# Turned blocks copied inside SBUF by the weights' queue, in a hybrid SSD and attention encoder block

## What is computed

```python
h = rms_norm(x, g_mix)
proj = h @ w_in                         # z, xbc, dt, q, k, v, gate_a, gate_b
y_ssm = mamba2_bidir(z, xbc, ...)       # conv, two scans, times silu(z), grouped rms_norm
q, k = apply_rope(rms_norm(q)), apply_rope(rms_norm(k))
y_attn = gqa_bidir_blocks(q, k, v)
merged = sigmoid(gate_a) * (y_ssm @ w_ssm_up) + sigmoid(gate_b) * (y_attn @ w_attn_up)
x = x + merged @ w_out
x = x + square(relu(rms_norm(x, g_mlp) @ w_mlp_in)) @ w_mlp_out
return rms_norm(x, g_final)
```

## Time and profile before

| | us |
|---|---|
| median of 3 runs | 1610.12 |
| lowest and highest | 1608.63, 1610.78 |
| the profiled execution's own time | 1609.39 |
| its span, first to last instruction | 1607.3 |
| PE busy in it | 1595.4 |
| DVE, ACT, POOL busy in it | 1278.8, 927.99, 79.2 |

### The profile page before, as it was taken

One profiled execution on the slowest core, in us unless ns is written; L12 is line 12 of the kernel. 1 busy time (PEld: TensorE's weight loads), 2 busy tenths in 40 slices (PEclk: granted clock), 3 DMA queues, 4 the chain that ended last, 5 costly groups with the idle time before them and its releaser, 6 DMA issues.

```text
span 1607.3 us, 20614 instructions
## 1 busy us (share of the span) xinstructions
PE 1595.4 (99%) x7984; PEld 1349.2 (84%) x7984; DVE 1278.8 (80%) x1521; ACT 928.0 (58%) x1264; POOL 79.2 (5%) x67
## 2 busy tenths in 40 slices
PE   9999999999999999999999999999999999999998
PEld 7888888888888888888888888888888888888886
DVE  7978877888767688876666667999899988998893
ACT  7665566665666545554445555665566655655562
POOL 3000000000000134000000000000000000000000
PEclk9999999999999999999999999999999999999999
DMA  7665656665688776545877875558645863686461
GB/s 272 202 201 184 201 183 211 197 198 185 196 244 238 231 225 200 172 145 181 244 265 235 278 228 178 181 171 266 188 133 200 275 192 123 204 281 214 143 244 53
DMA packets 144993, 327.93 MB, mean 204 GB/s; under 512 B 10944, under 2 KB 19328, under 8 KB 144768
## 3 DMA queue, kind: packets, MB, share of 16 engines
q1 hardware_dynamic: 129376, 302.21, 58.5%
q10 hardware_dynamic: 15520, 24.41, 5.2%
HBM read 316.55 MB, written 10.03 MB: 203 GB/s over the span
## 4 chain that ended last, share of the span: by engine, by line
PE 95%; DVE 2%; issue 1%; DMA 1%; ACT 0%; POOL 0%; POOLq 0%; SPq 0%; ACTq 0%
PE G L1835 17%; PE G L1836 17%; PE G L1837 17%; PE G L1844 13%; PE S L1844 7%; PE G L1848 6%; PE S L1835 4%; PE S L1836 4%; PE S L1837 4%; PE S L1848 4%; PE S L1962 1%; DMA raw<-in_w_in 1%; DVE wlo L1108 1%; PE S L1990 0%; PE S L1939 0%
## 5 line engine op out<-in xcount | busy, mean ns | idle before, releaser
L668 ACT ACTIVATE whi<-raw 128x1024 fp32r<-128x1024 f32 x395 | 416.6, 1059 | 396.4 <-PE G L1837 230.4
L1108 DVE TENSOR_TENSOR wlo<-raw,whi 128x1024 fp32r<-128x1024 f32 x395 | 483.3, 1238 | 132.1 <-ACT whi L668 130.5
L1835 PE MATMUL G<-whi,a_both 128*128 128x512 f32 x768 | 300.0, 391 | 2.5 <-DVE wlo L1108 2.0
L1837 PE MATMUL G<-whi,a_both 128*128 128x512 f32 x768 | 299.0, 389 | 0.0
L1836 PE MATMUL G<-wlo,a_both 128*128 128x512 f32 x768 | 299.0, 389 | 0.0
L1844 PE MATMUL G<-a_both,whi 128*128 128x512 f32 x640 | 201.5, 396 | 0.0
L1835 PEld LDWEIGHTS G<-whi,a_both 128*128 128x128 f32 x768 | 144.2, 188 | 34.0 <-issue 2.8
L1837 PEld LDWEIGHTS G<-whi,a_both 128*128 128x128 f32 x768 | 144.2, 188 | 30.2
L1836 PEld LDWEIGHTS G<-wlo,a_both 128*128 128x128 f32 x768 | 144.2, 188 | 28.9
L1848 PEld LDWEIGHTS G<-a_both,wlo 128*128 128x128 f32 x640 | 120.2, 188 | 28.3
L1835 PE MATMUL G<-whi,b_hi 128*128 128x512 f32 x342 | 133.5, 390 | 0.0
(11 more groups left out here) (313 smaller groups left out, 2689.1 us busy)
## 6 DMA issues: line engine op xcount, KB each, us to landing
raw<-in_w_in SPq DMA_DIRECT2D x208, 512.0 KB, 4.4
raw<-in_w_mlp_in SPq DMA_DIRECT2D x74, 512.0 KB, 4.6
raw<-in_w_mlp_out SPq DMA_DIRECT2D x74, 512.0 KB, 4.9
gates<-in_w_mlp_in SPq DMA_DIRECT2D x54, 512.0 KB, 4.2
gates<-in_w_mlp_out SPq DMA_DIRECT2D x54, 512.0 KB, 4.8
raw<-in_w_ssm_up SPq DMA_DIRECT2D x32, 512.0 KB, 3.8
raw<-in_w_attn_up SPq DMA_DIRECT2D x32, 512.0 KB, 4.5
raw<-in_w_out SPq DMA_DIRECT2D x32, 512.0 KB, 5.2
```

The lines of the kernel that those rows point to most:

```text
L668: act.activation(high(m), piece(n), ACT.Copy).then_inc(hi_made, 1)
L1108: dve.tensor_tensor(low(m), piece(n), high(m).bitcast(F32), ALU.subtract).then_inc(lo_made, 1)
L1835: pe.matmul(out_ap, hi[:, k, cols], w_hi, start=start, stop=False)
L1837: return pe.matmul(out_ap, lo[:, k, cols], w_hi, start=False, stop=stop)
```

## The change

The two functions on ACT are gone, and the tensor `block_rows` with them. SP copies square row i to group j with a transfer of its own, from SBUF to SBUF: 32 partitions of 1 KB each, 32 KB, sixteen for a round, in four groups of four (one group for each j). SP does a group behind the load of a piece: it keeps a table `BESIDE` of the side work of every piece and, after issuing the load of piece n, does what belongs to piece n-7. So a z round has its groups at p 5, 6, 7 and p 0 of the next window, rope at p 6, 7, 0, 1, merged and residual at p 0, 1, 2, 3. A group waits for `blocks_turned`, the first of a round also for `lined` (or, for rope, `r_lo`), which tells that the last round's squares have been read. The count `s_across` (256 a round) takes the place of `s_put` and `s_got`: ACT waits for it before it puts the squares in order, DVE before it turns the next round. ACT gets one more wait, at p 2 of `residual`, for `taken`.

```diff
+SP_LAG = 7
+        def across(rnd, j, src, dst):
+            d = BLOCK_ROUNDS.index(rnd)
+            sp.wait_ge(blocks_turned, d + 1)
+            for i in range(4):
+                sp.dma_start(dst[Q * j:Q * (j + 1), i, :, :, :].rearrange("p c b t -> p (c b t)"),
+                             src[Q * i:Q * (i + 1), j, :, :, :].rearrange("p c b t -> p (c b t)")
+                             ).then_inc(s_across, 16)
+        def zgate(p, j):
+            if p == 5 and j:
+                sp.wait_ge(lined, j)
+            if p >= 5:
+                across(TS_Z + j, p - 5, blocks, turned_to)
+        def zturned(p, j):
+            if p == 0:
+                across(TS_Z + j, 3, blocks, turned_to)
...
+        def merged(p, j):
+            if j + TS_MERGED in ON_PE:
+                return
+            if p == 0:
+                sp.wait_ge(lined, BLOCK_ROUNDS.index(j + TS_MERGED))
+            if p < 4:
+                across(j + TS_MERGED, p, blocks, turned_to)
...
                 sp.dma_start(dst, src).then_inc(landed[piece_slot(n)], 16)
+                if n >= SP_LAG:
+                    then, done_beside = BESIDE[n - SP_LAG]
+                    for name, at in done_beside:
+                        if name in table:
+                            table[name](then, at)
...
-        def put_blocks(rnd, src=blocks[:, :, :, :, :]):
-            d = BLOCK_ROUNDS.index(rnd)
-            act.wait_ge(blocks_turned, d + 1)
-            act.dma_start(block_rows[d], src.rearrange("p j c b t -> p (j c b t)")).then_inc(s_put, 16)
-        def get_blocks(rnd, dst=turned_to):
-            d = BLOCK_ROUNDS.index(rnd)
-            act.wait_ge(s_put, 16 * (d + 1))
-            if d:
-                act.wait_ge(lined, d)
-            rows = block_rows[d].rearrange("(i w) (j x) -> j w i x", i=4, j=4)
-            for j in range(4):
-                act.dma_start(dst[Q * j:Q * (j + 1), :, :, :, :].rearrange("w i c b t -> w i (c b t)"), rows[j]
-                              ).then_inc(s_got, 16)
...
-                act.wait_ge(s_got, 64 * (d + 1))
+                act.wait_ge(s_across, 256 * (d + 1))
...
             if p == 2:
+                act.wait_ge(taken[pp], pr + 1)
...
-                dve.wait_ge(s_put, 16 * d)
+                dve.wait_ge(s_across, 256 * d)
```

More of the change, by code:

```diff
@@ L253, in due_halves, with beside_pieces, window @@
     return blocks[:cut], blocks[cut:]
+SP_LAG = 7
+def beside_pieces():
+    beside = {}
+    def window(r, par, kind, idx, sides):
+        for p in range(PIECES):
+            beside[piece_number(r, par, p)] = (p, sides)
+    walk(None, window)
+    return beside
+BESIDE = beside_pieces()
 def previous(r, par):
@@ L454, in build @@
     ts_t, ts_hi, ts_lo = sem("ts_t"), sem("ts_hi"), sem("ts_lo")
-    blocks_turned, s_put, s_got, lined = sem("blocks_turned"), sem("s_put"), sem("s_got"), sem("lined")
+    blocks_turned, s_across, lined = sem("blocks_turned"), sem("s_across"), sem("lined")
     x_hi, x_lo = sem("x_hi"), sem("x_lo")
@@ L555, in build @@
     cum_rows = nc.dram_tensor("cum_rows", (2, HEADS, T), F32).ap()
-    block_rows = nc.dram_tensor("block_rows", (len(BLOCK_ROUNDS), P, TB * N), F32).ap()
     turned_wide = turned_to[:, :, :, :, :].rearrange("p i c b t -> p (c b) i t")
@@ L600, in rope_parameters, with rope, heads_in, residual @@
                          consts[:, 5 * P:9 * P]).then_inc(s_rope, 16)
+        def across(rnd, j, src, dst):
[13 more added lines that the diff above has]
+                across(TS_Z + j, 3, blocks, turned_to)
+        def rope(p, n):
+            if p == 6 and n:
+                sp.wait_ge(r_lo, n)
+            if p >= 6:
+                across(("rope", n), p - 6, rope_blocks(n), head_blocks)
+        def heads_in(p, n):
+            if p < 2:
+                across(("rope", n), p + 2, rope_blocks(n), head_blocks)
+        def merged(p, j):
[5 more added lines that the diff above has]
+                across(j + TS_MERGED, p, blocks, turned_to)
+        def residual(p, j):
+            if j + TS_X2 in ON_PE:
+                return
+            if p == 0:
+                sp.wait_ge(lined, BLOCK_ROUNDS.index(j + TS_X2))
+            if p < 4:
+                across(j + TS_X2, p, blocks, turned_to)
+        table = {f.__name__: f for f in (zgate, zturned, rope, heads_in, merged, residual)}
         def window(r, par, kind, idx, sides):
@@ L912, in zgate @@
                                        accum_out=z_ss[:, 2 * tb + gg:2 * tb + gg + 1]).then_inc(z_sq, 1)
-            if p == 6:
-                put_blocks(TS_Z + j)
         def zturned(p, j, pr, pp):
-            if p == 1:
-                get_blocks(TS_Z + j)
             if p == 5:
@@ L929, in rope @@
                                    ).then_inc(r_sq, 1)
-            if p == 7:
-                put_blocks(("rope", n), rope_blocks(n))
         def heads_in(p, n, pr, pp):
[L934 to L937, removed]
             if p == 5:
                 d = BLOCK_ROUNDS.index(("rope", n))
-                act.wait_ge(s_got, 64 * (d + 1))
+                act.wait_ge(s_across, 256 * (d + 1))
                 act.activation(by_block(head_parts(n)[0], 0, 4), heads_wide, ACT.Copy).then_inc(lined, 1)
@@ L990, in merged @@
         def merged(p, j, pr, pp):
[L991 to L994, removed]
             if p == (2 if j + TS_MERGED in ON_PE else 6):
@@ L998, in residual @@
         def residual(p, j, pr, pp):
[L999 to L1002, removed]
             if p == (2 if TS_X2 + j in ON_PE else 6):
```

## The result

| | before | after |
|---|---|---|
| median of the runs of this comparison, us | 1609.75 | 1626.51 |
| lowest and highest (4 runs each), us | 1608.63, 1610.78 | 1624.16, 1627.11 |
| the profiled execution's span, us | 1607.3 | 1625.2 |

The ratio is 1.0102, with a 95% interval from 1.0084 to 1.0119. The forecast was 1610.4 with a range up to 1613.9, and a chance of 0.11 for slower: it was wrong, and the time came out above its whole range.

The account below looks back on a forecast made before the run. PE was taken as the bound, with nothing removed on its path. The profiled 1609.39 us plus 0.3 us for PE in merged 2 gave 1609.7, plus 0.7 to the median 1610.4, range 1608.3 to 1613.9.

Parts of the forecast that it names:

- What bounds the kernel, and what goes: Whole kernel: PE busy 1595.4 of 1607.3 us; taking away ACT's issues and traffic wins at most 0.7 us.
- SP's issue of 0.47 us: SP's four copies after each load: 0.47 us an issue, near SP's loads of x, making a step 2.3 us.
- SP keeps up: SP's queue: a step of 2.3 us against 2.72 us for a piece on PE, so SP does not fall behind.
- behind the load of 773.7: Merged 0: the last group, issued behind that load, lands at 778 to 779, or 781; ACT uses it at 780.50.
- The working for merged 2: Merged 2: last group issued from about 821.5 to 823.3, landing by 827.1, so PE loses 0.3 us.
- Twelve rounds and more at nothing: Ordinary rounds: copies are in time, or half a us late on engines with room, and cost nothing.
- The copy's own time of 0.53 us a group: SP's queue: a group takes 0.53 us, a quarter of the 2.1 us for one round of gets.
- The load in a full queue: Merged 2: each load of x or out takes 1.4 us in the full queue, with 1.3 or 2.1 as alternatives.
- each us that it starts later, PE stands one more: Merged 2: no slack behind ACT's start at 826.80, so its delay passes to PE in full.
- Rival 1: Small transfers are dear: a group takes 2.1 us, PE stands 4.3 us in merged 2: 1614.4; chance 0.08.
- Rival 2: SP's issues of 1 us put loads 7 us late; PE loses 2 to 4 us in merged 2: 1613.5; chance 0.04.
- The list of what would show it: Signs across the trace: right if PE's pause at line 1856 is under 1 us, wrong at 3 us or more.

Follow-up runs that it names:

- e1: The changed kernel with SP copying inside SBUF only in the nine z and rope rounds, merged and residual going through device memory by ACT as before: 1609.43 us.
- e6: The changed kernel with all sixteen SP copies a round reading x from device memory in place of SBUF: 1618.99 us.
- e3: The changed kernel with each group of four SP copies made one 128 KB transfer, squares staying in their partitions: 1614.43 us.
- e5: The changed kernel with two copies of each group issued by SP and two by ACT one piece later: 1612.29 us.
- e9: The changed kernel with SP copying inside SBUF only in the three residual rounds, the others through device memory by ACT as before: 1615.85 us.
- e11: The changed kernel with SP_LAG 6 in place of 7, so every group stands one load earlier in SP's queue: 1615.73 us.
- e12: The kernel of e11 with merged 2 alone copied through device memory by ACT, as before the change: 1612.28 us.
- e2: The changed kernel with SP copying inside SBUF only in the six merged and residual rounds, z and rope through device memory as before: 1626.05 us.
- e8: The changed kernel with all sixteen copies a round issued by ACT, four a piece, in place of SP: 1612.42 us.

## Why the prediction was wrong, step by step

**What bounds the kernel, and what goes: right.** There was nothing to gain. With ACT's issues and 16 MB of traffic gone (e1, for nine rounds) the time did not move. ACT's queue fell to 8.68 MB, as said.

**SP's issue of 0.47 us: wrong in size, and it is the first step that failed.** It is 0.59 and 0.04 of pause, 0.63; a group is 2.4 us. The row that I took it from, SP's loads of x at 469 ns, and the gets read device memory; the copies read SBUF, and e6 shows that this is the difference. The load behind a group was overlooked: it costs 0.58 in place of 0.37. (One load behind a group took even 1.60.) By 0.63 the step is 3.1 us, over the 2.72 of a piece, and "SP keeps up" turns round. The upper bound of that paragraph, 4.5 us a step, held the truth, but was put aside as something of a full queue.

**"SP keeps up", by comparing a step with 2.72 us: wrong in kind, the second step.** e6 has the step of the forecast, 2.3 us, and loses 9 us. The mean pace is the wrong measure. SP's loads around a turn are bunched: it waits for DVE, which is turning, and then issued four loads in 5.5 us. The four groups lie exactly in this stretch. Without any pause four steps of 2.3 take longer than that, so the loads get later, and the last group with them.

**The last group "behind the load of 773.7": the same error, seen from the row.** I took the time of the fourth load from the trace of before and hung the group on it. The load itself moved, to 778.94. An instruction added ahead of a load moves that load: its old time is no bound for what follows it. The working for merged 2 did chain the issues, and came to 821.5 to 823.3 for the last group (its own terms, added up again, give about 820.3 to 822.8); but it began from a first load at its old time, and with 0.47. It is 830.12. "Twelve rounds and more at nothing" is right for nine.

**The copy's own time of 0.53 us a group: not refuted.** The copies land in a median of 3.0 us, beside the loads' 3.6 to 5.8; e3 and e5 move the same bytes at far less loss. The load in a full queue was 1.4 us in the sum; in e3, where the three loads of x and the first of out landed at 818.9, 820.3, 822.3 and 824.1, it is about 1.7 on the mean. This is a mis-sized term, small beside the first two.

**From ACT's delay to PE: "each us that it starts later, PE stands one more" was too simple.** ACT was 10.35 us late at the squares of merged 2, of which PE stood 4.5 us at line 1890. 2.5 us more it had lost already at low parts ahead of them, 1.7 to the half clock behind these (3.4 us of it), and 0.7 were there before the first copy; the last 1.0 I can't place. That stops also cost granted clock was no term of the sum, and it is some 5.8 of the 17.9 us. In none of the fully covered stretches that I had looked at had PE stopped, so no row had shown its price.

**The rivals.** Rival 1, dear transfers, gave 1614.4 and falls by e3 and e5. Rival 2, SP falls behind, is what happened: the loads are issued late, as its condition says. It had a chance of 0.04 and a price of at most 4 us. Both were too low for the same reason: it was tied to an issue of 1 us, and its room of 10 us was used by each round as if the round before had given it back. Merged and residual rounds follow each other every 22 us, and e9's squares are late by 2.9, 5.0 and then 6.2 us, 0.9 of it from before these rounds. The Trainium skill, "DMA: Bandwidth & Descriptors", section Issuing engines are not separate DMA queues, says that issuing from several engines saves only the time to initiate a transfer, which it calls usually small beside the transfer. Here an issue is 0.59 us beside a landing of 3.0, sixteen of them are 10 us of a round, and giving half of them to ACT (e5) saved 14.7 us. The measurement decides: for small transfers in a busy queue it is not small. The Trainium skill, "DMA: Bandwidth & Descriptors", section Bandwidth, calls transfers under 64 KB descriptor-dominated. Its figures are of loads issued by GpSimd, and the estimate that the prediction drew from them, 2.7 to 3.8 us for a group served one copy after another, is shown by no run: the four copies of e11's first group, issued 0.6 us apart, each landed 1.8 to 1.9 us after its issue, so none waited for the one ahead. The issue time is the same for 32 and 128 KB (e3), so here it was the count of issues that mattered and not their size.

**The list of what would show it.** Right: ACT's queue at 8.7 MB, no wait of ACT for squares in the z rounds, no wait of SP for ACT between 420 and 940 us. Wrong: PE busy about 1595 us and idle at no new place (1603.3, with three kinds of stops), issues at 0.3 to 0.5 us, the second load of out landed by 825 (it was issued at 826.21), ACT's start within 1 us of 826.8, and the pause at line 1856, which is 4.5 us and fell under "wrong, with the loads issued late".

## What to carry to other kernels

Before putting transfers into the queue that feeds the weights, lay its issues end to end from the last point at which it waited, with the added ones between them, and compare with the time that the same loads took there before, not with the mean pace of the matmuls. Price an issue by its source and destination, not by bytes, and count that the next load behind it gets dearer too. Where rounds follow each other, carry the lateness of one into the next, and add to each stop of PE what the clock takes behind it.

## What the runs showed of the hardware that I had not expected

- A DMA issue from SBUF to SBUF took SP 0.59 us whether it held 32 or 128 KB, and ACT 0.61 (32 KB) to 0.63 (128 KB); from device memory to the same place 0.42 (e6). A load right behind such copies took 0.58 (once 1.60), alone 0.37. At 64 KB the issue was 0.60.
- The copies are quick when nothing is ahead of them: the first group of e11's merged 0 landed after 1.8 us, the groups behind a load after about 3. Row of that group:

```profile
DMA to landing us min/median/max: 1.8/1.8/1.9
```

- PE's clock went from 2.4 to 1.2 GHz after some of the stops: after those of 1.9 and 4.5 us in the changed kernel for 3.4 us each, and for 6.8 us with that of 3.5 us, of which PE still stood for some 1.5. After the stops of 1.3 and 1.0 us in e12 and of 0.9 in e1 it stayed at full speed. In e3 it was 3.4 us behind a stop of 3.6, so 1.7 us more for a single stop. The length of a stop alone does not tell: in e2 a stop of 1.84 us was followed by no half clock, where 1.86 in the changed kernel was, and e2's stop of 3.5 us by 3.4 us of it and not 6.8.
- Half of the copies in each of two queues (e5) was the cheapest complete way with all fifteen rounds, 2.1 us above before; all in ACT's (e8) was 2.3, which these intervals can't tell apart.
